# Up-projection of a ConvGLU block: gate half and value half, one after the other or product by product in turn

## The reference

```python
SEQ, D_MODEL, D_FF, FFN_CONV_K = 512, 1024, 2816, 3
x = x + jnp.concatenate([u, att, y], axis=-1) @ w_out[i]
h = rms_norm(x, norm_ffn_g[i])
f = causal_dwconv(h @ w_up[i], ffn_conv_w[i], ffn_conv_b[i])   # 3 taps along the sequence
fa, fg = jnp.split(f, 2, axis=-1)                              # value half, gate half
x = x + (jax.nn.silu(fg) * fa) @ w_down[i]
```

## Time and profile before

| | |
|---|---|
| time, median of 3 runs | 717.38 us (717.37 to 717.59) |
| the profiled execution's own time | 717.7 us |
| its span, first to last instruction | 716.0 us |
| PE busy | 697.0 us, 97% |
| DVE busy | 545.4 us, 76% |
| ACT busy | 380.6 us, 53% |
| POOL busy | 141.8 us, 20% |
| mean DMA rate | 145 GB/s |

### The profile page before, as it was taken

One profiled execution on the slowest core, in us unless ns is written; L12 is line 12 of the kernel. 1 busy time (PEld: TensorE's weight loads), 2 busy tenths in 40 slices (PEclk: granted clock), 3 DMA queues, 4 the chain that ended last, 5 costly groups with the idle time before them and its releaser, 6 DMA issues.

```text
span 716.0 us, 9787 instructions
## 1 busy us (share of the span) xinstructions
PE 697.0 (97%) x3402; PEld 560.4 (78%) x3402; DVE 545.4 (76%) x852; ACT 380.6 (53%) x570; POOL 141.8 (20%) x114
## 2 busy tenths in 40 slices
PE   4999999999999999999999999999999999999998
PEld 4776888667666788788888888888888888888886
DVE  4368989988898947667667777876766866997895
ACT  6254655988878765633464343343343343654660
POOL 2000477944564402233410000000000000000000
PEclk9999999999999999999999999999999999999999
DMA  8731314211111141312234588656687547864552
GB/s 245 235 127 60 118 59 117 62 60 59 59 60 60 59 177 61 135 70 60 59 118 140 173 246 249 190 170 200 186 249 237 179 160 298 297 221 140 169 162 88
DMA packets 87554, 104.09 MB, mean 145 GB/s; under 512 B 6871, under 2 KB 65591, under 8 KB 87519
## 3 DMA queue, kind: packets, MB, share of 16 engines
q1 hardware_dynamic: 87375, 103.12, 45.9%
q10 hardware_dynamic: 144, 0.52, 0.2%
HBM read 87.10 MB, written 16.54 MB: 145 GB/s over the span
## 4 chain that ended last, share of the span: by engine, by line
PE 87%; ACT 7%; DVE 4%; issue 2%; DMA 1%; POOL 0%; DVEq 0%; ACTq 0%
PE bank L1767 75%; PE bank L1773 4%; PE bank L1787 2%; ACT tapped L1129 1%; ACT w_hi L934 1%; PE bank L1975 1%; DVE u_acc L622 1%; PE bank L2031 1%; PE bank L1951 1%; DVE xbcT L1427 1%; PE bank L1926 1%; DMA x_in<-in_x 1%; ACT prob L1052 1%; ACT dec L1099 0%; DVE prob L1406 0%
## 5 line engine op out<-in xcount | busy, mean ns | idle before, releaser
L1767 PE MATMUL bank<-h_hi,w_hi 128*128 128x512 f32 (+1 forms) x496 | 192.9, 389 | 0.0
L1767 PE MATMUL bank<-h_lo,w_hi 128*128 128x512 f32 (+1 forms) x496 | 189.9, 383 | 0.0
L1767 PE MATMUL bank<-h_hi,w_lo 128*128 128x512 f32 (+1 forms) x496 | 189.8, 383 | 0.0
L1767 PEld LDWEIGHTS bank<-h_hi,w_hi 128*128 128x128 f32 x496 | 93.2, 188 | 25.7 <-issue 7.8
L1621 DVE SCALAR_TENSOR_TENSOR f<-bank,prm,f 128x511 f32<-128x511 f32 x88 | 65.8, 748 | 60.7 <-ACT f L1182 55.2
L1767 PEld LDWEIGHTS bank<-h_hi,w_lo 128*128 128x128 f32 x496 | 93.2, 188 | 18.4
L1767 PEld LDWEIGHTS bank<-h_lo,w_hi 128*128 128x128 f32 x496 | 93.3, 188 | 17.3
L860 POOL TENSOR_TENSOR u_acc<-tapped,u_acc 128x511 f32<-128x511 f32 (+29 forms) x60 | 90.1, 1502 | 46.1 <-ACT tapped L1129 43.0
L1182 ACT ACTIVATE f<-bank,prm 128x512 f32<-128x512 f32 x44 | 34.2, 777 | 70.4 <-PE bank L1767 70.2
L640 DVE TENSOR_TENSOR w_lo<-w_raw,w_hi 128x2048 fp32r<-128x2048 f32 x24 | 55.6, 2316 | 8.9 <-ACT w_hi L934 8.7
L1767 PE MATMUL bank<-w_hi,g_parts 128*128 128x512 f32 x168 | 53.8, 389 | 0.0
(11 more groups left out here) (279 smaller groups left out, 1228.2 us busy)
## 6 DMA issues: line engine op xcount, KB each, us to landing
w_raw<-in_w_up SPq DMA_DIRECT2D x44, 512.0 KB, 6.1
w_raw<-in_w_in SPq DMA_DIRECT2D x34, 512.0 KB, 4.6
down_raw<-in_w_down SPq DMA_DIRECT2D x22, 512.0 KB, 5.4
weight_sums<-down_raw SPq DMA_DIRECT2D x11, 768.0 KB, 5.3
w_raw<-in_w_out SPq DMA_DIRECT2D x12, 512.0 KB, 4.5
weight_sums<-w_sum SPq DMA_DIRECT2D x11, 512.0 KB, 2.7
w_raw<-weight_sums SPq DMA_DIRECT2D x6, 768.0 KB, 6.0
down_raw<-weight_sums SPq DMA_DIRECT2D x5, 768.0 KB, 4.4
```

The lines of the kernel that those rows point to most:

```text
L1767: ins = pe.matmul(o, a, b, start=first and i == 0 and q == 0, stop=last and i == n - 1 and q == 2)
```

## The change

Chunk 0 stays. From chunk 1 on, a chunk waits for its weights and for both of its banks, and then each of the 24 products of weights and input is computed for the gate half and for the value half before the next product: 48 matmuls, alternating between the two banks. The same matmuls are done, on the same operands, and as many weight loads. ACT, DVE and SP run the same instructions in the same order. The last two matmuls of the chunk raise `acc_step`.

```diff
+            def both_halves(c, outs):
+                h, l = (w[:, c % NSLOT, :].rearrange("p (k s n) -> p k s n", k=KD, s=2)
+                        for w in (whi, wlo))
+                for kk in range(KD):
+                    for q, (w, m) in enumerate(((h, hhi), (h, hlo), (l, hhi))):
+                        for v, o in enumerate(outs):
+                            ins = pe.matmul(o, w[:, kk, v], m[:, kk, :], start=kk == 0 and q == 0,
+                                            stop=kk == KD - 1 and q == 2)
+                            if kk == KD - 1 and q == 2:
+                                ins.then_inc(acc_step, 1)
...
             for v in range(2):
                 pe.wait_ge(drained[FFN_BANK[2 + v]], ROUND0[2 + v])
-                channels(UP0 + 1, v, bank[FFN_BANK[2 + v]][:, :], range(KD)).then_inc(acc_step, 1)
+            both_halves(UP0 + 1, [bank[FFN_BANK[2 + v]][:, :] for v in range(2)])
...
                     for v in range(2):
-                        i = 2 * s + v
-                        pe.wait_ge(drained[FFN_BANK[i]], n + (ROUND0[i] + 1))
-                        channels(c, v, bank[FFN_BANK[i]][:, :], range(KD)).then_inc(acc_step, 1)
+                        pe.wait_ge(drained[FFN_BANK[2 * s + v]], n + (ROUND0[2 * s + v] + 1))
+                    both_halves(c, [bank[FFN_BANK[2 * s + v]][:, :] for v in range(2)])
```

## The result

| kernel | median | lowest to highest | executions |
|---|---|---|---|
| before | 717.51 us | 717.37 to 717.63 | 9 |
| changed | 719.62 us | 719.47 to 721.31 | 9 |

The ratio is 1.0035, 95% interval 1.0027 to 1.0043: 2.1 us slower. The profiled execution took 719.53 us with a span of 717.8; before it was 717.7 and 716.0, so 1.8 us lie between the two profiles.

A forecast was written before the change was run, and what follows sets the result against it. PE was taken to bound the kernel, never waiting from chunk 1 to the last product. 0 (distance) + 0 (loop) + 2.1 us (change of phase) on the median of 717.4 gave 719.5 us, range 718.4 to 721.4.

The forecast's parts named there:

- Distance: Start-to-start time of PE's matmuls: stays 0.2266 us though each writes another bank than the one before; cost 0.
- Both rivals on the distance: Alternating matmuls: distance shrinks, 706 us, chance 0.08; or grows by a few ns each, 722 to 725 us, chance 0.04.
- names no other term: Skill page's matmul distance, read as columns by clock plus 2.5 ns only: 215.8 ns; if alternation reached it, 708.5 us.
- The loop: Chunks before the last: ACT and DVE start 5.2 us later, yet PE never waits; cost 0, thinnest margin 0.6 us.
- The rival of waits in the loop: PE waits for `w_lo` up to four times, 0.1 to 0.4 us each, or step-1 rows land late: 720 to 721.2, chance 0.13.
- One sign: In the profile after, `sg` follows the gate's `f` by 2.6 us in every chunk, the value's `f` directly behind.
- The change of phase: Between chunk 21 and the down-projection: PE waits for bank 1, then for step 1's low parts, losing 2.1 us.
- `down_lo` for step 2: Low weights at the down-projection's step 2: ready at 620.3, PE wants them at 620.8, so no wait.
- The inputs: Sums, block loads and step-1 rows ahead of the change of phase: about 3 us later, but still in time.
- passes with 0.9: Step-1 rows land at 609.9, ACT wants them at 610.8: in time with 0.9 us left.
- The prediction's third rival: The loop waits too: PE waits for `w_lo`, or step-1 rows land late; 720 to 721.2 us, chance 0.13.
- The low weights for step 0: `w_lo` at the down-projection's start: done at 607.6, PE wants it at 607.88; any wait is part of the 2.1.

The follow-up runs named there:

- run 8: Changed kernel, but chunks 18 and 21 computed gate half first as before the change; 717.44 us.
- run 4: Changed kernel, all chunks from 1 on alternating, but ACT makes both halves' `f` before the high parts and `sg`; 717.33 us.
- run 10: Changed kernel, but in chunk 21 alone ACT makes both halves' `f` first, then step 1's high parts, then `sg`; 717.35 us.
- run 3: Kernel before the change, with only the last chunk, 21, alternating; 719.41 us.
- run 6: Changed kernel, with ACT also making the second half of step 1's high parts (0.95 us) ahead of chunk 21's value `f`; 720.36 us.
- run 1: Changed kernel, but the last chunk, 21, computed gate half first as before the change; 719.35 us.
- run 9: Kernel before the change, with only chunk 18 alternating; 718.37 us.
- run 2: Changed kernel, but the last two chunks, 20 and 21, computed gate half first as before the change; 719.09 us.
- run 7: Changed kernel, with step 1's second-half and step 2's high parts (2.8 us in all) also ahead of chunk 21's value `f`; 724.35 us.

## Why the prediction was right, point by point

**Distance: right.** 884 matmuls in the window of 200 us, and 717.44, 717.33 and 717.35 us in runs 8, 4 and 10 with 19, 21 and 21 alternating chunks. Were each of the 1000 matmuls dearer by 1 ns, they would be at 718.4. Both rivals on the distance are out. 226.6 ns stays, whichever bank the matmul ahead wrote. The 215.8 ns that the prediction took from the Trainium skill ("TensorE: Matmul & The Clock Gate", section "Back-to-back issue gap") is what that section gives for a matmul by itself; for a stream of weight loads and matmuls, which this kernel runs, it says that both set the spacing, and has some 131 ns for 512 columns. So "names no other term" was not right, and the rows agree with neither figure.

**The loop: right.** The timelines of ACT and DVE for chunk 8 in the changed kernel, A = 466.29:

```profile
466.29 0.78 ACT L1182 ACTIVATE f<-bank,prm 128x512 f32<-128x512 f32 x1 [4.96 <-PE bank L1789]
468.90 0.63 ACT L1189 ACTIVATE sg<-f 128x512 f32<-128x512 f32 x1 [1.83 <-DVE f L1621]
469.44 0.76 ACT L1182 ACTIVATE f<-bank,prm 128x512 f32<-128x512 f32 x1
```

DVE:

```profile
470.34 1.64 DVE L1621 SCALAR_TENSOR_TENSOR f<-bank,prm,f 128x511 f32<-128x511 f32 x2 [1.48 <-ACT f L1182]
472.13 0.69 DVE L1643 TENSOR_TENSOR g_raw<-f,sg 128x512 f32 x1
473.08 2.29 DVE L1596 TENSOR_TENSOR w_lo<-w_raw,w_hi 128x2048 fp32r<-128x2048 f32 x1 [0.26 <-ACT w_hi L1171]
```

`sg` follows at A + 2.6, the value's `f` at 3.15, `g_raw` at 5.8, and `w_lo` ends at 475.37, A + 9.1, as predicted behind an even chunk; behind chunk 7 it ended at A + 10.2 (predicted 10.3). PE had no wait. The rival of waits in the loop is out. One sign was put too strictly: `sg` does not follow the gate's `f` by 2.6 us in every chunk. It is 2.8 in chunk 7, and 4.2 in chunk 20 (596.76 to 600.99), where DVE is still at the late eleventh sums.

**The change of phase: right, by its own steps.** Predicted and measured:

| step | predicted | measured |
|---|---|---|
| gate's `f` (A) | 607.9 | 607.64 |
| `sg` | 610.3 | 610.02 |
| L1179 | 610.8 | 610.56 |
| value's `f` | 611.8 | 611.51 |
| bank 1 free | 614.1 | 613.83 |
| low parts ready | 615.2 | 614.97 |
| PE at step 1 | 615.4 | 615.02 |
| lost | 2.1 | 2.09 |

All of it, PE too, ran 0.3 earlier than I put it, which changes no difference. Runs 3, 10 and 6 show it as the cause: the last chunk alone brings it, another order on ACT in that chunk takes it away, and 0.95 more on ACT costs 1.0 more. `down_lo` for step 2 was ready at 617.68 + 2.28 = 619.96, and PE began step 2 at 620.61: it passed, as predicted.

**The inputs: right in their times, wrong in what I made of them.** First eleventh sum, the load of step 1's rows, and its row among the transfers, in the changed kernel:

```profile
596.41 0.69 DVE L1584 TENSOR_TENSOR w_sum<-down_raw 128x512 f32<-128x512 f32 x1 [1.71 <-DMA down_raw<-in_w_down]
```

SP:

```profile
604.54 0.43 SPq L789 DMA_DIRECT2D down_raw<-weight_sums  x1
```

The transfer, KB and us to landing:

```profile
down_raw<-weight_sums SPq DMA_DIRECT2D x1, 768.0 KB, 4.7
```

Landing was 609.2 (predicted 609.9), wanted at 610.56, and I wrote that it "passes with 0.9". It passes only because ACT is itself late. Against the 608.08 of before it is 1.1 late, and that is a loss of its own, hidden under the larger one. It came to light when run 1 took the larger away and the time stayed. The prediction named one cause for 2.1 us; the runs show two causes side by side, 2.1 by chunk 21 (run 3) and 1.0 by chunk 18 (run 9), or 2.0 and 1.8 in runs 1 and 2 with their slower load, and their maximum counts, not their sum: with both, the changed kernel takes what run 3 takes with one. The prediction's third rival had late rows as something on top of the 2.1. The low weights for step 0, put at their limit with 607.6, were done at 604.57 + 2.28 = 606.85.

**Left out: the clock.** Three of 14 executions of the changed kernel took 721.15 to 721.31 us at a mean granted clock of 0.997 to 0.998; the others were at 719.34 to 719.78 and 0.999 to 1.0. The prediction had no term for it. The difference, 1.8 us, would be some 9 matmuls at the 0.2 us that run 7 shows at 1.2 GHz. No profile caught such an execution, so this is inferred. A low mean clock doesn't by itself place the loss at the change of phase: one execution of run 10, whose profile has no wait there, took 718.61 us at a mean clock of 0.95.

**Open.** Why an issue of SP takes longer while instructions are transferred: the traces show that the two go together, not by what means. And what made the rows of run 2's profile land another 1.1 us later than its issue accounts for.

## What to carry to other kernels

Finishing two accumulators together instead of one after the other costs nothing on the matmul engine, but it takes the head start of the first one from everything behind it; what that is worth is decided where a chain has no next chunk to hide in, here at the change of phase, so trace the last chunk's chain instruction by instruction. When a late input "passes" because its reader has become late too, count it against the old reader's time: it is a second limit, and undoing the first gives back only what the first has more than the second (of 2.1 us about 1.1 by run 9's measure, and nothing in run 1, where the load was slow as well). A test that moves code out of a loop can also move when instructions are loaded; look at the transfers before you read its time. Where an engine serves both halves in order, put what frees an accumulator ahead of what only feeds the next phase; that took the loss away completely (717.35 against 717.37 us), though no version here beat the kernel before.

## What the runs showed of the hardware

- Writing another accumulator bank with every matmul costs nothing and wins nothing over a change at every 24th (0.2266 us in both).
- The granted clock fell to 1.2 GHz behind a wait of 4.2 us in the profile of run 7, and the mean clock was under full in all four of its executions. Behind the 1.4 us of the changed kernel the mean clock was lower in 3 of 14, behind that of run 3 in none of 7, behind the 1.3 and 2.4 us of the profiles of runs 1 and 2 in none of 8 each, behind the 2.3 us of run 6 in one of 5 (721.85 us). The Trainium skill ("TensorE: Matmul & The Clock Gate", section "The HAM clock gate") says that "the default state is throttled, and activity releases the throttle"; run 7 agrees: 1.2 GHz behind the wait, and the distance of 2.4 GHz again from 623.42, with PE at work throughout.
- At 1.2 GHz the distance was 0.427 us, just one column per clock (512 / 1.2 = 426.7 ns). At 2.4 GHz it is 226.6 against 213.3. The 13.3 ns are thus not a fixed price on each matmul; what they are these runs don't show.
- The issue of one and the same load took SP 0.43, 1.41 and 1.59 us in different kernels, and its landing 4.4 to 6.6 us. The two long ones stand beside a transfer of instructions on queue q8, as do all 17 of the down-projection's 528 loads whose issue took 0.62 us or more.
